# Stick-breaking attention: the projection groups woven into a step all stand between its transposes and its value products

## The reference, cut to what matters

```python
def stick_breaking(q, k, v):
    for i in range(L // BLOCK):
        s, e = i * BLOCK, (i + 1) * BLOCK
        z = einsum('bqhd,bkhd->bhqk', q[:, s:e], k[:, :e]) * scale
        mask = (arange(e)[None, :] < arange(s, e)[:, None])
        log_1m = where(mask, log_sigmoid(-z), 0.0)
        rest = cumsum(log_1m, reverse=True) - log_1m
        a = where(mask, exp(log_sigmoid(z) + rest), 0.0)
        outs.append(einsum('bhqk,bkhd->bqhd', a, v[:, :e]))

def odd_mixer(h, w_in, w_out):
    q, k, v = split(h @ w_in, 3)
    return stick_breaking(heads(q), heads(k), heads(v)).reshape(...) @ w_out
```

## Time and profile before

| what | before |
|---|---|
| median of 3 runs | 2414.18 us (2410.23 to 2414.76) |
| profiled execution, its own time | 2410.66 us |
| its span, first to last instruction | 2408.8 us |
| TensorE matmul busy | 2365.0 us, 98% of the span |
| VectorE, ScalarE, GpSimd busy | 46%, 35%, 38% |
| mean granted TensorE clock | 0.996 of full speed |

### The profile page before, as it was taken

The page is one execution under the profiler, slowest core; times in us unless marked ns, Lnnn a source line. Parts: engine busy times, 40 slices in busy tenths (PEclk is TensorE's granted clock), DMA queues, the critical chain, the costliest instruction groups (busy, mean ns, idle before and its releaser), DMA issues.

```text
span 2408.8 us, 37842 instructions
## 1 busy us (share of the span) xinstructions
PE 2365.0 (98%) x15330; PEld 2075.1 (86%) x15330; DVE 1107.5 (46%) x1672; ACT 847.3 (35%) x1314; POOL 919.2 (38%) x382
## 2 busy tenths in 40 slices
PE   7999899999999999999999999999999999999999
PEld 7888889999999999998988888766667888888887
DVE  4884443574452533555644525343474337422222
ACT  4324424432222333454322223443454324322222
POOL 4321124344444442222444444422224555444443
PEclk9999999999999999999999999999999999999999
DMA  5121112222222232111222222321212333222232
GB/s 174 69 71 36 67 59 97 71 91 101 88 87 88 87 110 71 53 38 70 81 96 102 87 96 96 107 70 53 88 53 88 121 106 105 98 94 93 99 105 87
DMA packets 33419, 208.08 MB, mean 86 GB/s; under 512 B 3706, under 2 KB 6420, under 8 KB 9240
## 3 DMA queue, kind: packets, MB, share of 16 engines
q1 hardware_dynamic: 29552, 202.00, 24.5%
q10 hardware_dynamic: 3752, 4.41, 0.6%
HBM read 204.27 MB, written 2.12 MB: 86 GB/s over the span
## 4 chain that ended last, share of the span: by engine, by line
issue 60%; POOL 23%; PE 16%; POOLq 1%; DMA 0%; ACT 0%; DVE 0%; SPq 0%; DVEq 0%; ACTq 0%
POOL wl L2480 23%; PE ps L392 14%; PE ps L345 1%; PE ps L327 1%; POOLq L2479 0%; POOLq L2484 0%; DMA raw<-in_w_all 0%; ACT L430 0%; ACT wh L430 0%; PE ps L488 0%; DVE X L463 0%; SPq L2447 0%; DVEq L463 0%; ACTq L429 0%
## 5 line engine op out<-in xcount | busy, mean ns | idle before, releaser
L2480 POOL TENSOR_TENSOR wl<-raw,wh 128x1024 fp32r<-128x1024 f32 x376 | 918.9, 2448 | 1473.1 <-ACT wh L430 1472.9
L430 ACT ACTIVATE wh<-raw 128x1024 fp32r<-128x1024 f32 x376 | 395.2, 1054 | 764.5 <-PE ps L392 498.4
L392 PE MATMUL ps<-Hh,wl 128*128 128x264 f32 (+2 forms) x1736 | 481.2, 326 | 0.0
L392 PE MATMUL ps<-Hl,wh 128*128 128x264 f32 (+2 forms) x1736 | 481.2, 326 | 0.0
L392 PE MATMUL ps<-Hh,wh 128*128 128x264 f32 (+2 forms) x1736 | 481.1, 326 | 0.0
L392 PEld LDWEIGHTS ps<-Hh,wh 128*128 128x128 f32 x1736 | 292.0, 188 | 28.4 <-issue 0.2
L392 PEld LDWEIGHTS ps<-Hh,wl 128*128 128x128 f32 x1736 | 291.3, 188 | 27.8
L392 PEld LDWEIGHTS ps<-Hl,wh 128*128 128x128 f32 x1736 | 291.3, 188 | 27.3
L345 PE MATMUL ps<-Hh,wh 128*128 128x264 f32 (+1 forms) x1056 | 282.7, 332 | 3.4 <-DVE arena L364 3.0
L345 PE MATMUL ps<-Hl,wh 128*128 128x264 f32 (+1 forms) x1056 | 258.3, 309 | 0.0
L345 PE MATMUL ps<-Hh,wl 128*128 128x264 f32 (+1 forms) x1056 | 257.9, 308 | 0.0
(11 more groups left out here) (252 smaller groups left out, 2826.4 us busy)
## 6 DMA issues: line engine op xcount, KB each, us to landing
raw<-in_w_all SPq DMA_DIRECT2D x188, 1024.0 KB, 4.8
X<-in_xT SPq DMA_DIRECT2D x4, 528.0 KB, 9.5
arena<-scratch ACTq DMA_DIRECT2D x2, 1024.0 KB
arena<-in_extra ACTq DMA_DIRECT2D x2, 528.0 KB
out<-X SPq DMA_DIRECT2D x1, 1024.0 KB, 4.3
out<-X SPq DMA_DIRECT2D x4, 256.0 KB, 2.0
arena<-in_extra ACTq DMA_DIRECT2D x2, 264.0 KB
cst<-in_consts SPq DMA_DIRECT2D x1, 448.0 KB, 11.1
```

The lines of the kernel that those rows point to most:

```text
L392: mm = pe.matmul(ps[:, 2 * j + h + bank, 0:c1 - c0], w[:, j, k, :], moving(x, blk, c0, c1), start=(at == 0 and part == 0), stop=(at == len ...
L430: act.activation(wh[:, j], raw[:, j // 2, :, P * (j % 2):P * (j % 2) + P], ACT.Copy).then_inc(hi_split, 1)
L2480: pool.tensor_tensor(wl[:, j], raw[:, j // 2, :, P * (j % 2):P * (j % 2) + P], wh[:, j].bitcast(F32), ALU.subtract).then_inc(split_ready[j ...
```

## The change

Only the table is changed: the groups that stood ahead of the turns come behind them, and the number of groups in each iteration stays.

```diff
--- before.py
+++ after.py
@@ -1648,7 +1648,7 @@
-        STICK_FILL = [(2, 2), (2, 4), (4, 2)]
+        STICK_FILL = [(0, 4), (0, 6), (0, 6)]
 
         def stick_pe(pe):
             d = stick_views()
```

## The result

The changed kernel takes 2441.09 us (median of 4 runs, 2440.41 to 2441.68) against 2414.40 us before (4 runs): **26.7 us slower**, a ratio of 1.0118 with a 95% interval of 1.0106 to 1.0130. The forecast was 2427.3 us, range 2419 to 2434, so the measured time lies outside it. The direction was right, and half of the size was missing.

A forecast was written before the change was run, and what follows sets the result against it. The prediction took TensorE, busy 98% of the span, to bound the kernel. Its terms, 14.8 - 1.7 + 0 + 0 = +13.1 us, on the median of 2414.18 gave 2427.3 us, range 2419 to 2434.

The forecast's parts named there:

- What bounds the kernel: In the attention stage's rounds TensorE is the bound, so every microsecond it idles is a microsecond of the kernel.
- Term 1: At fourteen unit ends inside blocks of six groups, the next group waits for VectorE's evacuation, 1.06 us each: +14.8 us.
- term 2: The 0.24 us wait already paid behind the turns with x = 2 goes, seven times: -1.7 us.
- Term 3: In iterations 1 to 20, one block start fewer, offset by turns directly behind scores: 0, bounds 2.2 us either way.
- Term 4: Earlier turns wait for VectorE's product; cover 1.3 us (x = 0), 2.3 (x = 1), x = 2 just fits: 0, bound 2.1 us.
- Nothing else is released later than its user needs it: Behind the turns in TensorE's round, copies come earlier, weight units are split four units ahead, no DMA moves: no cost.
- The rival of a second wait: Turns of x = 2 come late behind VectorE's chain, 0.5 to 1 us a round, 3.5 to 7 us more; chance 0.10.
- The clock rival: In the attention stage, the clock falls from full speed (1.00) with the new gaps; chance 0.04.
- A larger cover for the copies has nothing to hide: TensorE waits for ScalarE's copies only in iterations 21 to 24, which keep their order, so more cover gains nothing.

The follow-up runs named there:

- late_split: The changed kernel, with ScalarE waiting for VectorE's product before its split in iterations with x = 0 and x = 1; 2426.55 us, ratio 1.0072.
- x1_only: The kernel before, with the new order only in the iterations with x = 1; 2419.65 us, ratio 1.0039.
- x2_only: The kernel before, with the new order only in the iterations with x = 2; 2423.75 us, ratio 1.0052.
- x0_only: The kernel before, with the new order only in the iterations with x = 0; 2410.74 us, ratio 0.9994.
- before_late: The kernel before, with only ScalarE's wait for VectorE's product put ahead of the split; 2412.91 us, ratio 1.000.
- shift3: The kernel before, with the scores of step 0 computed four times; 2415.50 us, ratio 1.0007.
- x01: The kernel before, with the new order in the iterations with x = 0 and x = 1 together; 2435.67 us, ratio 1.0098.
- tail_moved: The run tail, with the last unit's split moved from iteration 21 to iteration 23; ratio 1.0002 to the kernel before.
- lo_first: The changed kernel, with VectorE's low part of the output (L1770) ahead of the scans of its iteration; 2430.77 us, ratio 1.0071 to before.
- tail: The kernel before, with the groups moved behind the turns only in iterations 21 to 24; ratio 1.0001.
- shift1: The kernel before, with the scores of step 0 computed twice; 2415.49 us, ratio 1.0003.

## Why the prediction was half right

The sum had one half of the change right, the gaps, and left the other half out, so that 2441.1 us came out above the range.

- **What bounds the kernel:** right. Every wait of TensorE in the stage came out as time: 26.8 us in the stage, 26.7 in the median. That the two agree so closely has a little luck in it: the median of before happened to fall on runs that lost time to the clock outside the stage, as all runs of after did (mean granted clock 0.994 in each, against 0.996 in the profiled execution of before).
- **Term 1, the uncovered evacuation, and term 2:** right. The rows show 0.89 us of idle time fourteen times (the last one 1.00), where I had said 0.8 to 0.9, and late_split, which isolates them, 13.5 us, or 12.6 without the longer wait that its own edit makes, in place of 13.1. x1_only and x2_only, with the gaps alone, add up to 7.5 + 5.6 = 13.1.
- **Term 3, changes of the kind of work:** right. x0_only, which has it alone, in six of the twenty iterations, came out at -0.2 us in the stage, and x1_only and x2_only leave nothing over for it beside the gaps.
- **Term 4, the turns that come earlier:** here the prediction failed. It took each product's end from durations of before, 1.06 us for x = 0, and found a cover of 1.3 us. The cover was right; the product took 3.21 us, 2.15 longer than assumed, which is 0.87 more than the cover of 1.28, and the turns waited these 0.87. The term for it stood at 0 and measured 6 x 0.87 = 5.2 us. For x = 2, where the cover was said to be about nothing, no wait came, as counted.
- **"Nothing else is released later than its user needs it":** wrong twice. I looked only at what comes later. ScalarE's copy came *earlier* behind the scores, and with it the split and GpSimd's subtraction, 2.84 us behind the scores (1010.91 to 1013.75) in place of 4.04 (1000.76 in the earlier trace rows to 1004.80), which put GpSimd on top of the product. In the kernel before it had started just behind the product's end at 1005.88, as these rows of its timeline show:

```profile
1004.80 1.06 ACT L430 ACTIVATE wh<-raw 128x1024 fp32r<-128x1024 f32 x1
...
1005.93 2.37 POOL L2480 TENSOR_TENSOR wl<-raw,wh 128x1024 fp32r<-128x1024 f32 x1 [13.23 <-ACT wh L430]
```

  And I left out that the value products of x = 0 also wait for L1770, which lies behind the scans on VectorE: 6 x 1.39 = 8.3 us that no term of the sum had.
- **The rival of a second wait** had the right kind of mechanism, VectorE's chain being late for the turns, but named x = 2, and the price of 0.5 to 1 us a round was less than half of the 2.26 us that a round paid.
- **The clock rival:** granted clock 1.00 in the stage, as forecast, with waits of 1.5 us at most. Of the two runs with a wait of 2.38 us, before_late saw the clock fall behind it (to 0.79) and late_split did not (1.00). The chance of 0.04 was my estimate: no run shows the clock below 1.00 behind the new gaps of 0.89 us. Row of the kernel after, one stretch over the stage (columns as in the earlier trace rows):

```profile
933.00:1142.00 209.00, 179.43 (x1669) 160.44 (x1670) 119.03 (x140) 89.32 (x135) 38.01 (x15) 1.00 0.11 36
```

- **A larger cover for the copies has nothing to hide:** right, and more so than I thought: behind the sigmoids it was no larger cover at all.

## What to carry to other kernels

Before an order on one engine is moved, list what comes *earlier* through it, and lay GpSimd's instructions over those of VectorE that work in SBUF, first of all those with two SBUF operands: a duration from the old trace holds only for the old neighbours (the product took 1.06 us before and 3.21 beside GpSimd's subtraction). Work that fills TensorE's time is cover for two things, the buffer that is being emptied (0.89 us of wait when the cover was gone) and the result that is awaited (0.87 us); if it is taken from one place, check the wait that stood behind it there. If several consumers wait for one long queue, ask for each semaphore in front of a moved instruction, not only for the one that the change is about.

## What the runs showed of the hardware

**VectorE and GpSimd on SBUF.** In the kernel after, VectorE's product and scan, with two operands in SBUF, that started behind GpSimd's subtraction ended 0.9 us after GpSimd's end: the product at 1018.19, GpSimd at 1014.91 + 2.36 = 1017.27, and these 0.92 us are nearly the product's whole normal length of 1.06. From these two numbers it looks as if the product had hardly run before GpSimd's end; that is an estimate, no row shows it. In x1_only, VectorE's scan had started first, and GpSimd's row was the longer one instead (3.01 us against 2.36). L1770, with one operand in PSUM, was not held there (0.66 us within GpSimd's 3.01). The trace of before has many more such pairs outside the stage. On line 2427, an addition of two operands in SBUF, all 13 that began while GpSimd's subtraction ran took 1.33 to 2.93 us, and the 11 others 0.69; on line 2419, a product of the same size with one operand in PSUM, the 13 that began in such a time took 0.69 like the rest. Two operands in SBUF weren't needed everywhere: line 636, a TENSOR_SCALAR with one tensor in SBUF, normally takes 0.55 us and took 1.15 to 2.26 in the five cases where it began beside GpSimd.

**The clock elsewhere.** The spans outside the attention stage differ between the profiles, by up to 7.1 us (2239.2 before, 2246.3 in x2_only). What goes with them is the granted clock in two places, where it falls during a set of matmuls with 4 rows (L1914) or up to 15 us behind it: one set stands in the stage ahead of the mLSTM's (from 1583.7 us in the kernel before), one in the mLSTM stage itself (from 1648.7). From 20 us ahead of the first set I cut 140 us into stretches of 4 us and summed length times (1 - clock), a rough measure of the time lost; it gives 3.4 us in the profiles of before, late_split, before_late and shift3, 5.1 in x1_only, x01 and tail_moved, 6.8 after the change and in x0_only, 8.5 in lo_first, tail and shift1, and 10.2 in x2_only. The span less the stage less this sum lies between 2233 and 2237 us in all of them. Rows of x2_only from the second place (columns as in the earlier trace rows); two of the five stretches show a clock of 0.50, though TensorE was busy for all 4.00 us of each:

```profile
1659.00:1663.00 4.00, 4.00 (x15) 2.97 (x14) 0.00 (x0) 1.95 (x2) 0.00 (x0) 0.66 0.74 262
1663.00:1667.00 4.00, 4.00 (x14) 3.09 (x13) 0.42 (x1) 0.39 (x1) 0.00 (x0) 0.50 0.00 0
1667.00:1671.00 4.00, 4.00 (x19) 3.23 (x19) 0.53 (x2) 0.49 (x2) 0.00 (x0) 0.99 0.00 0
1671.00:1675.00 4.00, 4.00 (x8) 0.95 (x6) 0.99 (x3) 0.95 (x1) 2.34 (x1) 0.87 0.00 0
1675.00:1679.00 4.00, 4.00 (x9) 2.72 (x9) 0.00 (x0) 1.02 (x1) 0.00 (x0) 0.50 0.00 0
```

Two runs move the place by doubling work: the scores of step 0 twice, and four times.

> The kernel before with the scores of step 0 computed twice: one set of score matmuls more (1.03 us), nothing else. It moves all that follows by 1.03 us. In the seven profiles so far the spans outside the attention stage differ by up to 7 us, and the granted clock after the mLSTM stage's products with 4 rows (L1914) is at its lower level for stretches of different length at the same place of the work. Theory E (how long the clock stays low there depends on when the place is reached): the time does not rise by 1.0 us but differs from the kernel before by some 1 - 3.5 to 1 + 7 us, and the clock rows at 1580 to 1690 account for it. Rival: 1.0 us, with the spread of before.

> The same with the scores of step 0 computed four times: 3.1 us more work. Theory E: the difference to the kernel before is not 3.1 us; together with shift1 the two differ by something other than 2.1 us. Rival: 3.1 us.

Measured: 2415.49 and 2415.50 us against 2414.15, ratios 1.0003 (0.9994 to 1.0013) and 1.0007 (0.9998 to 1.0017). The stages with their extra work took 170.5 and 172.4 us, yet both kernels come out alike. In its profile the first lost 8.5 us to the clock and the second 3.4. The times do not decide between theory E and its rival: in us the intervals are -1.4 to 3.1 and -0.5 to 4.1, and the rival's 1.0 and 3.1 lie within them. The single runs show more. The kernel before ran 61 times beside the variants: 24 runs took 2409.6 to 2412.0 us, with a mean granted clock of 0.995 or 0.996, and 37 took 2413.8 to 2416.7 us, with 0.994; none lay between. So one and the same kernel meets either case. That the moment at which the place is reached decides it, and what sets the length of the low stretch, is not shown and stays open. For the reader it means that this kernel's time moves by some 4 us, in x2_only by 7, for a reason that has nothing to do with the waits of the edit, and that the median of before reads 2411.6 or 2414.3 by which group holds the middle run: compare the stage first.
